# State-space heads: the backward exponents go to ScalarE as Relu of a negated spread decay; convolution activations go to ScalarE too, and a weight split leaves the inner norm

## The reference, cut to what matters

```
qk = jax.nn.silu(centred_dwconv(qk, conv_w, conv_b))          # first block
q = heads(q) * M_HEAD_DIM ** -0.5
...
xbc = jax.nn.silu(depthwise_conv_centered(xbc, conv_w[i], conv_b[i]))   # second block
a_cum = jnp.cumsum(a_dt, axis=-1)
seg = a_cum[..., :, None] - a_cum[..., None, :]
decay = jnp.exp(jnp.where(lower, seg, -jnp.inf))
mix = cb[:, :, None] * decay
y_diag = jnp.einsum("bgrcls,bcsgrp->bclgrp", mix, xdt)
...
x = x + mixed @ w_out[i]
h = rms_norm(x, norm2_w[i])                                   # the inner norm
g, u = jnp.split(h @ w_up[i], [D_FF_2], axis=-1)
```

## Time and profile before

| | |
|---|---|
| median of 3 runs | 2185.26 us (2176.16 to 2187.72) |
| profiled execution | 2196.37 us, span 2194.6 us |
| PE busy | 2032.9 us, 93% |
| DVE busy | 1524.1 us, 69% |
| ACT busy | 999.6 us, 46% |
| granted PE clock, mean | 0.97 |

### The profile page before, as it was taken

One profiled execution on the slowest core, in us unless ns is written; L12 is line 12 of the kernel. 1 busy time (PEld: TensorE's weight loads), 2 busy tenths in 40 slices (PEclk: granted clock), 3 DMA queues, 4 the chain that ended last, 5 costly groups with the idle time before them and its releaser, 6 DMA issues.

```text
span 2194.6 us, 37133 instructions
## 1 busy us (share of the span) xinstructions
PE 2032.9 (93%) x15578; PEld 1909.9 (87%) x15578; DVE 1524.1 (69%) x2774; ACT 999.6 (46%) x1459; POOL 22.3 (1%) x36
## 2 busy tenths in 40 slices
PE   4899999989998999999999988999899989997998
PEld 4898888989988988899899967787899977887998
DVE  7887676677658877676665468765666688755665
ACT  3553454444444543554444333554544334554444
POOL 2000000000001000000000000000000000000000
PEclk7999999999999999999999999999999999999999
DMA  8455434548743555335475534222455333223553
GB/s 320 139 203 197 174 116 170 178 175 298 255 154 124 193 203 190 131 142 176 151 253 189 183 123 146 87 98 75 166 188 192 116 133 118 97 78 116 195 196 109
DMA packets 52770, 358.98 MB, mean 164 GB/s; under 512 B 5995, under 2 KB 8651, under 8 KB 9980
## 3 DMA queue, kind: packets, MB, share of 16 engines
q1 hardware_dynamic: 52412, 356.51, 45.6%
q10 hardware_dynamic: 192, 0.10, 0.0%
HBM read 355.41 MB, written 1.08 MB: 162 GB/s over the span
## 4 chain that ended last, share of the span: by engine, by line
PE 77%; DVE 16%; ACT 4%; issue 2%; DMA 1%; ACTq 0%; SPq 0%; DVEq 0%
PE projected L428 31%; PE projected L1442 19%; PE mixed L428 7%; PE mixed L1442 6%; DVE cacc L1861 3%; DVE w_lo L353 2%; PE mixed L1645 2%; PE mixed L1561 1%; PE mixed L502 1%; DVE nrm L963 1%; PE mixed L480 1%; PE mixed L568 1%; DVE w_lo L1380 1%; PE mixed L1550 1%; PE mixed L489 1%
## 5 line engine op out<-in xcount | busy, mean ns | idle before, releaser
L353 DVE TENSOR_TENSOR w_lo<-raw,w_hi 128x1024 fp32r<-128x1024 f32 x340 | 409.3, 1226 | 239.6 <-ACT w_hi L668 237.9
L668 ACT ACTIVATE w_hi<-raw 128x1024 fp32r<-128x1024 f32 x338 | 350.5, 1055 | 381.5 <-PE projected L428 312.8
L428 PE MATMUL projected<-u_hi,w_hi 128*128 128x256 f32 x1728 | 490.6, 284 | 27.8 <-DVE u_lo L874 27.8
L428 PE MATMUL projected<-u_lo,w_hi 128*128 128x256 f32 x1728 | 484.8, 281 | 0.0
L428 PE MATMUL projected<-u_hi,w_lo 128*128 128x256 f32 x1728 | 484.3, 280 | 0.0
L428 PEld LDWEIGHTS projected<-u_hi,w_hi 128*128 128x128 f32 x1728 | 330.4, 191 | 35.1 <-issue 34.4
L1380 DVE TENSOR_TENSOR w_lo<-raw,w_hi 128x1024 fp32r<-128x1024 f32 x204 | 245.9, 1223 | 153.3 <-ACT w_hi L1709 153.0
L428 PEld LDWEIGHTS projected<-u_hi,w_lo 128*128 128x128 f32 x1728 | 329.9, 191 | 0.0
L428 PEld LDWEIGHTS projected<-u_lo,w_hi 128*128 128x128 f32 x1728 | 329.0, 190 | 0.3
L1442 PE MATMUL projected<-u_hi,w_hi 128*128 128x256 f32 x992 | 283.2, 286 | 34.3 <-DVE w_lo L1380 34.3
L1709 ACT ACTIVATE w_hi<-raw 128x1024 fp32r<-128x1024 f32 x204 | 210.9, 1054 | 158.3 <-PE projected L1442 140.0
(11 more groups left out here) (369 smaller groups left out, 4085.4 us busy)
## 6 DMA issues: line engine op xcount, KB each, us to landing
raw<-in_stream_dram SPq DMA_DIRECT2D x324, 1024.0 KB, 4.9
w_mod<-in_first_ada_dram SPq DMA_DIRECT2D x8, 1024.0 KB, 15.1
band<-bias_rows SPq DMA_DIRECT2D x1, 3072.0 KB, 14.8
x<-in_xT_dram SPq DMA_DIRECT2D x1, 1024.0 KB, 4.8
out_dram<-uf SPq DMA_DIRECT2D x4, 256.0 KB, 2.5
tri<-in_tri_dram SPq DMA_DIRECT2D x2, 384.0 KB, 4.1
c<-in_c_dram SPq DMA_DIRECT2D x1, 512.0 KB
mask<-in_mask_dram SPq DMA_DIRECT2D x1, 384.0 KB, 25.5
```

Source lines behind the costliest of these rows:

```text
L353: eng.tensor_tensor(part(w_lo, step, half), raw_half(step, half), part(w_hi, step, half).bitcast(F32), ALU.subtract).then_inc(s_lo_dve, 1)
L428: m = pe.matmul(out, a, b, start=start and n == 0, stop=stop and n == 2, **kw)
L668: act.activation(part(w_hi, step, half), raw_half(step, half), ACT.Copy).then_inc(s_hi, 1)
```

## The change

- Second block, heads: the selector that spreads the decay is negated. DVE forms only the two forward pieces, as max(column - spread, 0), with add and max. ACT forms the two backward pieces as Relu(-spread + column) straight from PSUM, with the column as bias, waits for itself, and takes Exp with scale -1 over all four. PE now waits before `bc` of head i for Exp of head i - 2 (`s_ee`), since ACT reads the bank too.
- Both blocks: the silu of a convolution becomes one Silu on ACT, straight into its target; the tanh and DVE's two operations go. The convolution writes alternately to two tiles (`sth`), and DVE waits for the Silu two steps back. The factor of q goes into the score product, whose `tensor_tensor` becomes a `scalar_tensor_tensor`.
- The inner norm: `("wo2", 8 * l + 7)` is no longer held, so `("wg", 0)` is split at that step. In its place `("wu", 0)` is split in the norm, half before and half after, and left out at `("wg", 0)`.

```diff
             elif kind == "qk_silu":
                 act.wait_ge(s_cacc, N + 1)
-                act.activation(cth[:], cacc[:], ACT.Tanh, scale=0.5).then_inc(s_cth, 1)
+                act.activation(qkT[:, 2 * i:2 * i + 2, :], sth[i % 2][:], ACT.Silu).then_inc(s_qk, 1)
...
+                if N >= 2:
+                    dve.wait_ge(s_qk, N - 1)
+                conv = sth[i % 2]
...
-            elif kind == "qk_silu":
-                dve.wait_ge(s_cacc, N + 1)
-                scale = 0.5 * (MD ** -0.5 if i < 4 else 1.0)
-                dve.wait_ge(s_cth, N + 1)
-                link(dve.scalar_tensor_tensor(out=cacc[:], in0=cth[:], scalar=1.0, in1=cacc[:],
-                                              op0=ALU.add, op1=ALU.mult))
-                dve.tensor_scalar(qkT[:, 2 * i:2 * i + 2, :], cacc[:], scale, None, ALU.mult).then_inc(s_qk, 1)
-                dve.wait_ge(s_qk, N + 1)
...
-                    ins = dve.tensor_tensor(W[:, at:at + t1 - t0], W[:, at:at + t1 - t0],
-                                            MB[0][:, s * T + t0:s * T + t1], ALU.mult)
+                    ins = dve.scalar_tensor_tensor(out=W[:, at:at + t1 - t0], in0=MB[0][:, s * T + t0:s * T + t1],
+                                                   scalar=MD ** -0.5, in1=W[:, at:at + t1 - t0],
+                                                   op0=ALU.mult, op1=ALU.mult)
...
-HELD2 = [("wd", FP * l + FP - 1) for l in range(DEPTH - 1)] + [("wo2", 8 * l + 7) for l in range(DEPTH)]
+HELD2 = [("wd", FP * l + FP - 1) for l in range(DEPTH - 1)]
...
-        step = ("wd", FP * l - 1) if i == 0 else ("wo2", 8 * l + 7)
-        return due(CHUNKS2, step)
+        return due(CHUNKS2, ("wd", FP * l - 1)) if i == 0 else [CHUNKS2.index(("wu", FP * l))]
+
+    def rounded_at(step):
+
+        later = [("wu", FP * l) for l in range(DEPTH)]
+        return [n for n in due(CHUNKS2, step) if n < len(CHUNKS2) and step not in HELD2 and CHUNKS2[n] not in later]
...
                     if i >= 2:
-                        pe.wait_ge(s_ex, SH * l + i - 1)
+                        pe.wait_ge(s_ee, SH * l + i - 1)
...
-                    act.activation(sel_r[:], ident[0:SH, 0:SH], ACT.Copy).then_inc(s_ach, 1)
+                    act.activation(sel_r[:], ident[0:SH, 0:SH], ACT.Copy, scale=-1.0).then_inc(s_ach, 1)
...
                 act.wait_ge(s_cacc, ENDS["cacc"] + n + 1)
-                act.activation(cth[:], cacc[:], ACT.Tanh, scale=0.5).then_inc(s_cth, 1)
+                act.activation(xbc[:, 2 * i:2 * i + 2, :], sth[n % 2][:], ACT.Silu).then_inc(s_xbc, 1)
...
                     act.wait_ge(s_ex, SH * l + i + 1)
-                    act.activation(W[:, i % ABUF, :], W[:, i % ABUF, :], ACT.Exp).then_inc(s_ee, 1)
+                    for (d, s, t0, t1), at in zip(PIECES[2:], PLACE[2:]):
+                        ins = act.activation(W[:, i % ABUF, at:at + t1 - t0], MB[i % 2][:, d * T + t0:d * T + t1],
+                                             ACT.Relu, bias=cols[:, 0, s, d, i:i + 1])
+                    link(ins)
+                    act.activation(W[:, i % ABUF, :], W[:, i % ABUF, :], ACT.Exp, scale=-1.0).then_inc(s_ee, 1)
...
-                convolve(l, cacc, zc[:, n % 2], V2_CW, V2_CB, 2 * i, TAPS2, XBC).then_inc(s_cacc, 1)
+                if n >= 2:
+                    dve.wait_ge(s_xbc, n - 1)
+                convolve(l, sth[n % 2], zc[:, n % 2], V2_CW, V2_CB, 2 * i, TAPS2, XBC).then_inc(s_cacc, 1)
                 dve.wait_ge(s_cacc, ENDS["cacc"] + n + 1)
-                dve.wait_ge(s_cth, ENDS["cth"] + n + 1)
-                link(dve.scalar_tensor_tensor(out=cacc[:], in0=cth[:], scalar=1.0, in1=cacc[:],
-                                              op0=ALU.add, op1=ALU.mult))
-                dve.tensor_scalar(xbc[:, 2 * i:2 * i + 2, :], cacc[:], 0.5, None, ALU.mult).then_inc(s_xbc, 1)
-                dve.wait_ge(s_xbc, n + 1)
...
-                    for (d, s, t0, t1), at in zip(PIECES, PLACE):
+                    for (d, s, t0, t1), at in zip(PIECES[:2], PLACE[:2]):
                         ins = dve.tensor_scalar(W[:, i % ABUF, at:at + t1 - t0], MB[i % 2][:, d * T + t0:d * T + t1],
-                                                cols[:, 0, s, d, i:i + 1], 0.0, ALU.subtract, ALU.min)
+                                                cols[:, 0, s, d, i:i + 1], 0.0, ALU.add, ALU.max)
```

More of the change, by code:

```diff
@@ L254, in first_block @@
     s_cacc = sem("conv_sum_ready")
-    s_cth = sem("conv_tanh_ready")
     s_qk = sem("mlstm_qk_ready")
@@ L391, in first_block @@
                  "s_hid": s_hid, "s_hidh": s_hidh, "s_hf": s_hf, "s_th": s_th, "s_zc": s_zc, "s_cacc": s_cacc,
-                 "s_cth": s_cth, "s_asc": s_asc, "s_am": s_am, "s_ae": s_ae, "s_an": s_an, "s_at": s_at, "s_pt":
+                 "s_asc": s_asc, "s_am": s_am, "s_ae": s_ae, "s_an": s_an, "s_at": s_at, "s_pt":
                  s_pt, "s_av": s_av, "s_o": s_o, "s_oh": s_oh, "s_var": s_var, "s_rstd": s_rstd, "s_small": s_small,
@@ L920, in vector @@
                        .then_inc(s_gcol, 1)
+                if N >= 2:
+                    dve.wait_ge(s_qk, N - 1)
+                conv = sth[i % 2]
                 for half in range(2):
                     tile = 2 * i + half
-                    dve.tensor_scalar(cacc[:, half, :], zc[:, i % 2, half, 0:T], conv_w(l, 0, tile),
+                    dve.tensor_scalar(conv[:, half, :], zc[:, i % 2, half, 0:T], conv_w(l, 0, tile),
                                       vec[:, V_CB + tile:V_CB + tile + 1], ALU.mult, ALU.add).then_inc(s_dve, 1)
@@ L929, in vector @@
                         ins = dve.scalar_tensor_tensor(
-                            out=cacc[:, half, :], in0=zc[:, i % 2, half, tap:tap + T],
-                            scalar=conv_w(l, tap, 2 * i + half), in1=cacc[:, half, :], op0=ALU.mult, op1=ALU.add)
+                            out=conv[:, half, :], in0=zc[:, i % 2, half, tap:tap + T],
+                            scalar=conv_w(l, tap, 2 * i + half), in1=conv[:, half, :], op0=ALU.mult, op1=ALU.add)
                         if tap < TAPS1 - 1 or half == 0:
@@ L1196 @@
         "uh": 16 * DEPTH, "hid": DEPTH * FP, "hidh": DEPTH * FP, "hf": DEPTH * FP, "th": DEPTH * FP, "zc": 8 * DEPTH,
-        "cacc": 8 * DEPTH, "cth": 8 * DEPTH, "asc": 2 * SLOTS * DEPTH, "am": 2 * SLOTS * DEPTH, "ae": 2 * SLOTS *
+        "cacc": 8 * DEPTH, "asc": 2 * SLOTS * DEPTH, "am": 2 * SLOTS * DEPTH, "ae": 2 * SLOTS *
         DEPTH, "an": 2 * SLOTS * DEPTH, "at": 2 * SLOTS * DEPTH, "pt": 2 * SLOTS * DEPTH, "av": 2 * SLOTS * DEPTH,
@@ L1299, in second_block @@
     sems = k["sems"]
-    (s_hi, s_lo_dve, s_used, s_u, s_uf, s_uh, s_hid, s_hidh, s_hf, s_th, s_zc, s_cacc, s_cth, s_asc, s_am, s_ae, s_an,
+    (s_hi, s_lo_dve, s_used, s_u, s_uf, s_uh, s_hid, s_hidh, s_hf, s_th, s_zc, s_cacc, s_asc, s_am, s_ae, s_an,
      s_at, s_pt, s_av, s_o, s_oh, s_var, s_rstd, s_small, s_landed, s_dve, s_act, s_one16, s_dw_hi, s_dw_lo, s_x) = (
         sems[n] for n in ("s_hi", "s_lo_dve", "s_used", "s_u", "s_uf", "s_uh", "s_hid", "s_hidh", "s_hf", "s_th",
-        "s_zc", "s_cacc", "s_cth", "s_asc", "s_am", "s_ae", "s_an", "s_at", "s_pt", "s_av", "s_o", "s_oh", "s_var",
+        "s_zc", "s_cacc", "s_asc", "s_am", "s_ae", "s_an", "s_at", "s_pt", "s_av", "s_o", "s_oh", "s_var",
         "s_rstd", "s_small", "s_landed", "s_dve", "s_act", "s_one", "s_gw_hi", "s_gw_lo", "s_pre"))
@@ L1715, in scalar @@
             kind, N, l, i = local(step)
-            if step in CHUNKS2 and step not in HELD2:
-                for n in due(CHUNKS2, step):
+            if step in CHUNKS2:
+                for n in rounded_at(step):
                     round_weights(n)
```

## The result

The changed kernel takes 2169.8 us (median of 13 runs, 2167.5 to 2180.4), the kernel before 2185.3 beside it (13 runs). The ratio is 0.9938, 95% interval 0.9921 to 0.9955: 13.5 us less (9.8 to 17.3). The two medians differ by 15.5 us, inside that interval. A second timing on another chip, beside other kernels, gave 0.9938 again, interval 0.9911 to 0.9966. Forecast were 2168.7 us and 16.6 us less. The total is close, but one of its terms, that of the heads, was wrong, and much of this text is about that one.

A forecast was written before the change was run, and what follows sets the result against it. PE, busy 93% of the span, was taken as the bound, so DVE work counts only where PE waits for DVE. Terms 10.4 + 7.0 - 1.4 + 0.6 = 16.6 us took 2185.3 to 2168.7, range 2158 to 2179.

The forecast's parts named there:

- The norm, 10.4 forecast: Inner norm: PE starts 5.2 us sooner, after the first u_lo pair; 10.4 us in two layers (9.8 to 16.0).
- rival (a): Inner norm: the clock stays up, 8.0 for 5.2 us twice, 22.2 in all, 2163 us; chance 0.10.
- The second block's convolutions, 7.0 forecast: Second block's convolutions: z 1 starts 3.5 us sooner per layer, 7.0 in all (4.4 to 7.8).
- The first block, 0.6: First block's convolution stage: 0.3 us less at the first two v, 0.6 in all (0 to 0.6).
- The heads, -1.4 forecast: State-space heads: a net loss of 0.7 us per layer, -1.4 in all (0 to -6).
- PE loses 1.4: Head 4: Exp of head 2 ends at 1371.9 instead of DVE's pieces at 1370.49, so PE waits 1.4 us more.
- The 0.7 given back at `group_norm`: Ahead of group_norm: the square PE waits for comes 0.7 us sooner, the 0.5 at head 11 included.
- I cost it at nothing: Convolutions: a new table load of 1.28 us ahead of z 0's tanh, once a layer, costs nothing; 1.3 if it shows.
- (b): Inner norm: PE doesn't start sooner, something else in ACT's or DVE's order holds it; 6.2 in all, 2179 us; chance 0.08.
- (d): Heads: the wait for Exp is felt at every head because ACT bounds the stage; 2212 us; chance 0.05.
- (c): Convolutions' gain is taken back by the added load and worse stalls in the heads; about 2175 us; chance 0.05.
- (e): Heads: Relu isn't in the table that holds Exp, two loads of 1.28 us a head; 2249 us; chance 0.02.

The follow-up runs named there:

- kernel 6: Changed kernel plus Exp's table loaded early at the step of z 1 and head 4 moved behind the product of ak2 0; ratio 0.9897 to before.
- kernel 1: Kernel before with only the inner norm's split changed; ratio 0.9964 to before, 7.9 us less.
- kernel 2: Kernel before with only the convolutions of both blocks changed to Silu; ratio 0.9968 to before, 7.0 us less.
- 3: Kernel before with only the heads changed, two of four pieces as Relu on ACT; ratio 1.0023 to before.
- experiment 4: Changed kernel plus one instruction that loads Exp's table early, at the step of z 1; ratio 0.9934 to before.
- 8: Changed kernel with Exp's table loaded early and each head's Relu pair run twice; ratio 0.9963 to before.
- kernel 9: Changed kernel with heads put back, head 4 moved behind ak2 0, head 11 behind aq2 1 with group_norm after it; ratio 0.9893 to before.

## Why the prediction came out as it did

**The norm, 10.4 forecast: right.** Idle time 2 x 5.13 = 10.3, ended by `u_lo`. I took the product behind it to be as long as before. Its first 48 matmuls took 7.12 and 7.07 us in the two layers after and 7.95 and 7.84 before, 1.6 in all: a part of rival (a), which had 5.6. It is not firm: with the new norm the other kernels have 5.7 to 8.4, and only the 5.7 (layer 1 of kernel 6) is what (a) wanted.

**The second block's convolutions, 7.0 forecast: right.** PE's first matmul of the `wdt` product in layer 0, before and after:

```profile
1288.05 0.47 PE L1442 MATMUL mixed<-u_hi,wdt_hi 128*32 128x256 f32 x1
```

```profile
1275.72 0.47 PE L1441 MATMUL mixed<-u_hi,wdt_hi 128*32 128x256 f32 x1
```

From there to `z` 1 are 60.3 us before (1288.05 to 1348.32) and 56.3 after; layer 1 goes from 60.0 to 56.4. Every kernel with Silu has 56.2 to 56.4 in both layers, and every one without it 60.0 to 60.3. That is 4.0 + 3.6 = 7.6. **The first block, 0.6: right.** Between the stop of PE that ends at 64.98 and the one that ends at 81.11 lie 16.13 us before and in kernel 1, and 15.82 in the changed kernel (64.89 to 80.71) and in kernel 2; the like in layer 1 goes from 16.04 to 15.72: 0.6 in all.

**The heads, -1.4 forecast: this is the term that was mis-sized.** Measured are 195.4 - 191.0 = 4.5 us in layer 0, and in layer 1 1974.71 - 1779.24 = 195.5 against 2001.85 - 1805.73 - 5.13 = 191.0, again 4.5: -9.0, outside the bounds of 0 to -6. (Those bounds were generous as it was: by the forecast's own figures, slower Relus at heads 4 and 11 and nothing given back at `group_norm` make 2.3 a layer, -4.6.) Step by step:
- The chain to head 4, "PE loses 1.4": measured 1.91 - 0.61 = 1.30 wherever no load was in it (3, 4). The Relu pair is 0.73, as summed from two other lines. The 0.7 given back at `group_norm`, head 11's wait included, is measured as 0.45 + 0.50 against 1.75: 0.8. These steps hold.
- "I cost it at nothing": the load was expected at `z` 0's tanh. It came with Exp, behind the first Relu pair, on the chain to head 4, and added 1.27. Experiment 2 shows the same load free with the old heads, experiment 4 shows it free when early. The failed step is the place of the load, and the edit that made the place matter was another one than the edit that made the load.
- No term at all for the clock behind a stop. I had priced the clock in the norm, where PE stood long, and not at head 4, where a stop of 2.0 us was forecast. Behind 1.91 us the windows show 0.64 and 0.71, behind 3.18 us 0.51. From `bc` of head 4 to `bc` of head 5 PE takes 7.96 us before, 9.4 to 9.5 behind the stop of 1.91, and 10.7 to 11.0 behind that of 3.2: 1.4 to 1.6 and 2.8 to 3.1 us more, as much as the stop. Experiment 6 removes the stop, and the clock stays at 1.00.

These steps add up: in the changed kernel 2.57 us more of idle time at head 4, 0.8 less at head 11 and `group_norm`, and 3.0 of slow clock make 4.8, measured 4.5; in kernels 3 and 4 1.30 - 0.8 + 1.5 = 2.0, measured 1.8 to 2.3.

The sum by traces is 10.3 + 1.6 + 7.6 + 0.6 - 9.0 = 11.1 us, inside the timed interval (9.8 to 17.3). The median after came within 1.1 us of the forecast partly by luck: the gains were 2 us above their terms, the loss 7.6 above its own, which makes 5.5 less than forecast, and the medians happen to lie 4.4 further apart than this sum.

**The rivals.** (b) and (d) fall with experiments 1 and 8. (c) is the one that the traces bear out: it said that an added load and worse stalls in the heads would take back what the convolutions give, and they took 9.0 against 8.2 given. Its 10.4 us in all is close to the 11.1 of the traces; the timed 13.5 lies midway between it and the forecast's 16.6, and its interval excludes neither. I gave it 0.05, which was too little. (e) falls: Relu brings no load of its own. The Trainium skill, ScalarE: Activation LUTs, Table sets, has relu in every set, and the rows at 1346.06 agree: the pair ran 0.73 us with Silu's table in place, ahead of the load. The rule of the Trainium skill, ScalarE: Activation LUTs, Rules for kernel authors, to keep relu off ScalarE was set aside in the forecast. The pieces themselves take about the same on either engine here (467 and 366 ns on ACT, 481 and 342 on DVE); the trace agrees with the rule only where a head is waited for, 1.30 us at head 4 and 0.45 at head 11.

**A better version.** The changed kernel with an early table load and head 4 later has the shortest way in the trace, 5.7 us a layer below the changed kernel, and 0.9897 against 0.9938 of before; moving head 11 too gives 0.9892. The intervals of these and of the changed kernel overlap slightly, and they ran on different chips, so that both beat the kernel before is shown, and that they beat the changed one is shown by the traces alone. Whether the heads on ACT are worth keeping once head 4 is moved, the times can't tell: 0.9897 against 0.9893 for kernel 9, the best with the heads put back. In the trace up to `att2` it is 88.4 against 89.4 us, 1.0 a layer for keeping them.

## What to carry to other kernels

Here an activation table was loaded at the first instruction that needed it, so ask of each new function which later one no longer finds its table, and whether that one stands on a chain; a preload in a wait cost nothing here. Price a stop of PE as the stop and the slow clock behind it: here the second part was as large as the first already at 2 us, and one product of 5.7 us put in front of the waiting step removed both. When several edits go in together, look for a cost that one creates and another puts on the path: load alone 0, heads alone 2.0 us, both 4.5 us a layer.

## What the runs showed of the hardware

- Behind an idle stretch of PE at head 4, over the next 2.5 to 3.9 us, the granted clock was 1.00 after 0.61 us, 0.64 to 0.71 after 1.91, 0.51 after 3.18 and 0.50 after 4.20. The slow stretch cost 1.4 to 1.6 us behind 1.91, 2.8 to 3.1 behind 3.2, and no more, 2.3 to 2.4, behind 4.20 (both layers each).
- The same product behind the same stop of 2.1 us was granted 1.00 in one layer or execution and 0.81 in the next. The first `xbc` product of layer 1 and of layer 0 in the changed kernel's windows:

```profile
1714.36:1723.19 8.83, 8.83 (x34) 7.41 (x35) 5.24 (x11) 2.77 (x5) 0.00 (x0) 0.81 0.00 0
1268.93:1276.07 7.14, 7.14 (x34) 6.22 (x35) 5.49 (x16) 2.88 (x6) 0.00 (x0) 1.00 0.01 2
```

  In the kernel before it was the other way round (8.83 in layer 0, 7.14 in layer 1). What decides it stays open; it is 1.7 us of scatter a layer.
- With no stop of PE in between, 48 matmuls of a product in the feed-forward of layer 0 took 5.65 us in the profile of the kernel before and 5.44 in all the others.
- Two Relu of 256 and 128 columns from PSUM with a pointer bias take 467 and 366 ns, the pair 0.73 us; the same pieces on DVE 481 and 342 ns.
- Tanh and Relu run without a load with the table that Silu brought; Exp after it takes one of 1.28 us.
